# Local attention: two projection tiles in front of the third block's product with the values, the value rows copied behind the first exponents

## The reference, cut to what matters

```python
k_sh, v_sh = shared_kv(h, kv_norm, w_kv)          # 2 key/value heads of 64
q = (x @ w_q).reshape(b_, nb, WINDOW, 2, 8, 64)   # 16 query heads, nb = 4 blocks of 128
scores = einsum('bnqkgd,bnskd->bnkgqs', q, band(k)) * 64 ** -0.5   # block and the one before it: 256 keys
scores = where(valid, scores - slopes * dist, -inf)
m = maximum(max(scores), sink)
e = exp(scores - m)
probs = e / (sum(e) + exp(sink - m))
out = einsum('bnkgqs,bnskd->bnqkgd', probs, band(v))
return out @ w_o
```

## Time and profile before

| What | before |
|---|---|
| profiled execution, us | 2219.96 |
| its span, us | 2218.2 |
| median of the runs, us | 2217.85 |
| TensorE matmul, busy us (share of the span) | 2095.2 (94%) |
| TensorE weight load | 1669.1 (75%) |
| VectorE | 1340.3 (60%) |
| ScalarE | 859.3 (39%) |
| GpSimd | 228.0 (10%) |
| mean granted TensorE clock | 0.981 |

### The profile page before, as it was taken

The page is one execution under the profiler, slowest core; times in us unless marked ns, Lnnn a source line. Parts: engine busy times, 40 slices in busy tenths (PEclk is TensorE's granted clock), DMA queues, the critical chain, the costliest instruction groups (busy, mean ns, idle before and its releaser), DMA issues.

```text
span 2218.2 us, 24826 instructions
## 1 busy us (share of the span) xinstructions
PE 2095.2 (94%) x9958; PEld 1669.1 (75%) x9958; DVE 1340.3 (60%) x1924; ACT 859.3 (39%) x1297; POOL 228.0 (10%) x239
## 2 busy tenths in 40 slices
PE   8999989999999999999999999999998889999897
PEld 6777777778778878877787788777776567768675
DVE  4566655664566557556736755444445668787774
ACT  4322324442343435544424434432333344444342
POOL 2122221000000200000000001000000122120201
PEclk9999999999999999999999999999999899999998
DMA  5211112443342211134433333111101223222221
GB/s 176 67 48 48 48 48 86 139 137 123 114 138 90 100 48 39 57 104 153 135 112 124 114 105 114 54 42 38 38 29 51 81 67 100 86 82 80 105 86 48
DMA packets 55011, 191.63 MB, mean 86 GB/s; under 512 B 6000, under 2 KB 6320, under 8 KB 54768
## 3 DMA queue, kind: packets, MB, share of 16 engines
q1 hardware_dynamic: 54896, 190.04, 26.3%
HBM read 187.92 MB, written 2.10 MB: 86 GB/s over the span
## 4 chain that ended last, share of the span: by engine, by line
PE 75%; DVE 15%; ACT 6%; issue 2%; POOL 1%; DMA 0%; SPq 0%; DVEq 0%; ACTq 0%
PE PS L307 19%; PE PS L311 18%; PE PS L310 18%; PE PS L419 2%; DVE wlo L1798 2%; PE PS L892 2%; PE PS L866 2%; PE PS L867 2%; PE PS L314 2%; PE PS L317 1%; PE PS L318 1%; ACT whi L1178 1%; ACT s_s L1424 1%; PE PS L881 1%; PE PS L527 1%
## 5 line engine op out<-in xcount | busy, mean ns | idle before, releaser
L307 PE MATMUL PS<-nhi,whi 128*128 128x512 f32 x1456 | 605.8, 416 | 32.6 <-DVE wlo L1798 12.3
L311 PE MATMUL PS<-nhi,wlo 128*128 128x512 f32 x1456 | 576.2, 396 | 0.0
L310 PE MATMUL PS<-nlo,whi 128*128 128x512 f32 x1456 | 575.7, 395 | 0.0
L1798 DVE TENSOR_TENSOR wlo<-raw,whi 128x1024 fp32r<-128x1024 f32 x339 | 418.9, 1248 | 248.1 <-ACT whi L1178 247.5
L1178 ACT ACTIVATE whi<-raw 128x1024 fp32r<-128x1024 f32 x339 | 351.5, 1051 | 197.1 <-PE PS L307 147.8
L307 PEld LDWEIGHTS PS<-nhi,whi 128*128 128x128 f32 x1456 | 278.7, 191 | 112.6 <-DVE wlo L1798 20.1
L311 PEld LDWEIGHTS PS<-nhi,wlo 128*128 128x128 f32 x1456 | 277.6, 191 | 61.5
L310 PEld LDWEIGHTS PS<-nlo,whi 128*128 128x128 f32 x1456 | 279.1, 192 | 53.0 <-issue 2.6
L2570 POOL TENSOR_TENSOR diag<-diag,sqb 128x512 f32<-128x512 f32 (+1 forms) x56 | 73.3, 1309 | 1220.2 <-ACT sqb L1187 1137.6
L307 PE MATMUL PS<-hh_f,whi 128*128 128x512 f32 x352 | 138.7, 394 | 0.0
L311 PE MATMUL PS<-hh_f,wlo 128*128 128x512 f32 x352 | 138.0, 392 | 0.0
(11 more groups left out here) (349 smaller groups left out, 3379.4 us busy)
## 6 DMA issues: line engine op xcount, KB each, us to landing
raw<-in_stream SPq DMA_DIRECT2D x339, 512.0 KB, 3.5
dc<-in_decay SPq DMA_DIRECT2D x4, 1024.0 KB, 5.7
hT<-in_xT SPq DMA_DIRECT2D x8, 256.0 KB, 7.2
out<-hT SPq DMA_DIRECT2D x8, 256.0 KB, 2.1
ctx_f<-in_ctx SPq DMA_DIRECT2D x1, 1024.0 KB, 6.7
ab_h<-in_filt_out SPq DMA_DIRECT2D x8, 128.0 KB, 2.9
mask<-in_masks SPq DMA_DIRECT2D x1, 512.0 KB, 8.7
cs_m<-in_rope SPq DMA_DIRECT2D x1, 512.0 KB, 4.7
```

The costliest lines, as they stand in the source:

```text
L307: op = e.matmul(out, hi, xh, start=first, stop=False)
L310: e.matmul(out, hi, xl, start=False, stop=False)
L311: return e.matmul(out, lo, xh, start=False, stop=last)
L1798: e.tensor_tensor(m.wlo[:, c % HL, :], m.raw[:, c % RAW, :], m.whi[:, c % HL, :].bitcast(F), SUB).then_inc(*s.w_lo.tick(c))
```

## The change

A list `SWA_TILES` gives how many tiles of `pr` are issued at each step n: 2, 2, 1, 1, 0, 0, 2, 0, 0. It is used by TensorE, ScalarE and VectorE. `values_of_rows` is no longer a part of `pr` on ScalarE and is issued at the end of round -1.

```diff
+SWA_TILES = [2, 2, 1, 1, 0, 0, 2, 0, 0]
@@ in swa() of tensor_program, scalar_program and vector_program
-            for n in range(9):
-                next(pr, None)
-                if n < 4:
+            for n in SWA_TILES:
+                for _ in range(n):
                     next(pr, None)
                 next(y, None)
                 next(x, None)
             for g in (y, x, pr):
                 run(g)
@@ in swa() of scalar_program
-        def value_rows():
-            yield from w.steps(KD)
-            values_of_rows()
...
             if i < 0:
-                pr = value_rows()
+                pr = w.steps(KD)
...
             for g in (y, x, pr):
                 run(g)
+            if i < 0:
+                values_of_rows()
```

## The result

The changed kernel takes 2240.63 us (median of 5 runs, 2240.59 to 2241.49), the kernel before 2217.85 (5 runs, 2216.4 to 2222.15): a ratio of 1.0099, 95% interval 1.0084 to 1.0113. It is slower by 22.8 us; +20 was forecast. The profiled executions stand 20.6 us apart in their spans (2238.8 and 2218.2).

What follows compares the result with a forecast made beforehand. The chain round ScalarE and VectorE, not TensorE, was taken to bound the local attention. Terms -1.6 + 12.0 - 0.2 = +10.2 us, plus +10 for the clock, made +20: median 2238, range 2232 to 2245, 8 in 10 2227 to 2246.

Steps and rivals of the forecast that it cites:

- The chain before: Local attention rounds: waits go round ScalarE and VectorE, 14.89 us a round; TensorE's two block waits cost nothing.
- The rival "faster": Scores don't wait for VectorE's query product; rounds shorter by ScalarE's 1.0 us, value rows bring 4.2: 2208; chance 0.04.
- Part 1 and 2: Rounds 0 to 5: split leaves ScalarE's chain, -1.1 us; late query product enters, round 17.3 instead of 14.9, +2.4.
- eight steps for nine: Eight tiles are taken in nine steps, so the query product, VectorE's ninth, falls behind scaling and low part.
- Part 3: Value rows leave pair 0's exponents: pair 1's exponents come 4.2 us earlier, of which 1.6 is gained at the next scores.
- The 4.9 us for the eight exponents: Pair 0, value rows moved: the eight exponents run on from 797.70 and are done 4.9 us later.
- Part 4: Six new TensorE gaps of 3.1 us bring the half clock to the scores behind: 1.65 us each, +10.
- Ten of ten: TensorE's timeline: each of ten gaps of 2.59 to 3.84 us has half clock in it or within 1.4 us behind.

Runs made afterwards that it cites:

- e6: Kernel before with value rows behind the exponents of pair 0 and both splits of the chunk after next at a round's first tile: 2204.62 us.
- e4: Changed kernel with 12 identity matmuls on TensorE before the wait for the query product in rounds 1 to 6: 2226.63 us.
- e2: Changed kernel with the value rows copied in their old place, so the tile list alone: 2240.11 us.
- e3: Changed kernel with a ninth projection step in n = 6, so the query product comes behind the low split, ahead of four scalings: 2217.34 us.
- e5: Kernel before with only the query product of pairs 2 to 7 moved to the round's end on VectorE: 2240.97 us.
- e1: Kernel before with only the value rows moved behind the eight exponents of pair 0: 2213.94 us.
- e7: Changed kernel with both splits of the chunk after next at the first tile of rounds 0 to 5, query product still last: 2226.6 us.
- e8: Kernel before with value rows behind the exponents, early splits, and the new tile list on TensorE alone: 2204.55 us.

## Why the prediction was right

- **The chain before.** That TensorE's waits before the third and fourth block weren't in the chain is shown by e6: taking the splits out of ScalarE's and VectorE's queues shortened the rounds by 0.7 us until TensorE itself was the bound, and the moved tiles then brought 0.13. The rival "faster" took ScalarE's 1.0 off a round and left this bound out.
- **Part 1 and 2.** 17.3 us a round were forecast with the clock up, 17.43 and 17.49 measured (e4, e2). What is missing lies between the scores and the exponents, 7.27 in e4 for the forecast's 7.1. The gap was to be 3.1 and is 3.4. The step that carried the forecast, eight steps for nine, is shown by e3 and e5: one more step takes the loss away, one late query product makes it.
- **Part 3.** The first exponents of pair 1 and the scores of pair 2 came as forecast (-4.2 and -1.5). In e1, where nothing follows to eat the 4.2, 2.7 of them reached the end of the stage. The 4.9 us for the eight exponents is a slip: without copies among them they and the sink's took 4.05 (797.08 to 801.13), which is what the working's next figures count with.
- **Part 4.** The mechanism is shown by e4. Its size was too small: four of six slow stretches were double, and cost 2.9 to 3.0 instead of 1.65, so the stage lost 26.3 and not 20.2 us. The time came out near the forecast because the later stages had fewer slow stretches than in the run before: the distance between the two traces is 25.7 us at the first gap behind the stage (980.58 and 1006.30), 23.2 at 1394.77, 21.6 at 1669.65 and 20.6 at 2166.56. Nothing in the change explains that; all later work was only shifted in time. So the size of +20 was partly luck, with two errors of some 6 us, in the stage and outside it, that cancel. In the stage the slow stretches rose from 3.4 to 34.1 us, a price of 15 us where +10 was forecast.
- **All executions.** The split doesn't rest on two profiled executions alone. Each execution has a span and a mean granted clock on record; span times clock is an estimate of what it would take at full clock, and the rest is the clock's price (the clock has three digits, so each is good to 1 us). On the mean the price is 42.8 us in the 38 executions of the kernel before and 52.0 in the five of the changed one, and the rest 2174.8 and 2187.1: +9.2 and +12.3, where the forecast has +10 and +10.2. This is over the whole span, where the later stages give back part of what the doubles took.
- **Ten of ten** was too strong. The gap of 3.39 us before 840.15 in e2 had no slow stretch; nor had the gaps of 2.63 and 2.62 us before 1417.93 and 1691.26 in the changed kernel itself, whose twins before both had one.

The rule of the Trainium skill ("TensorE: Matmul & The Clock Gate", section "Why this matters for your kernels") is not to leave idle gaps between bursts, or the clock goes back to half. These traces agree in ten of the eleven gaps of 3.4 us (changed kernel, e2). Its guideline for the length of a gap is too lax here, as gaps of 2.32 us brought the half clock in five of five cases (e5) and gaps of 2.23 to 2.31 in three of six (e7); gaps of 1.7 to 1.8 did in none of six (e3).

The spread of 14 us between the executions of e6 comes from the clock: its granted mean is 0.987 in the fastest (span 2197.9) and 0.980 in the slowest (2211.8), and span times clock is 2168 to 2170 us in all six.

What stays open: why a slow stretch is single or double, as no run here sets the moment at which one begins; and why e6 and e8 lose less to the clock outside the stage than the kernel before. On the mean the price is 34.9 and 35.9 us in their 13 executions against 42.8, and in the profiled execution of the kernel before only 1.7 us of the price lies in the stage.

## What to carry to other kernels

When a generator's steps are recounted, count what hangs on the last one: here eight steps for eight tiles left a ninth, the hand-over to the next round, behind everything else in an in-order queue. A wait on an engine that isn't in the chain of waits is no target: look for what the chain goes through (a weight split among the exponents, value rows among them) and take that out. A new gap on TensorE can cost twice: here 2.5 us a round for the wait itself and 1.5 to 3.0 for the lower clock behind it, as what ran there was work the others wait for.

## What the runs showed of the hardware

- TensorE work that nobody needs can make a kernel faster: 12 matmuls of the identity a round, 2.7 us of work in a gap of 3.4, took 14 us off 2240.6.
- The half clock comes with a gap often, not always: at 3.4 us in ten of eleven cases (six of the changed kernel, five of e2), at 2.2 to 2.3 in eight of twelve (five of e5, six of e7, one of e2), at 1.7 to 1.8 in none of six (e3). The last is no safe length: four of the ten gaps of 1.5 to 2.13 us elsewhere in the kernel before had it. It then lasted 3.4 or 6.8 us, and the cost to a round was 1.4 to 1.8 or 2.9 to 3.0.
- Profiled executions of two programs that differ by 0.14 us at the end of the attention (e6, e8) ended 14.6 us apart, with 48 and 79 us at half clock; their medians are 0.07 apart. One program alone spreads as far (e6, 2199.73 to 2213.57). For this kernel a few us of difference need many runs of each side, and the granted clock of each run says how much of a difference is the clock.
